# Hybrid decoder step on one core: the down projection of 15 pairs of ff tiles as seven products, with weights combined on the chip

## The reference, cut to what matters

```python
D_MODEL = 1024
SEQ = 2048
D_FF = ((8 * D_MODEL + 3 * 256 - 1) // (3 * 256)) * 256      # 2816 = 22 tiles of 128
...
    h = _rmsnorm(x, g_pre_ffn) * (1.0 + sc_f) + sh_f
    gate, up = jnp.split(jnp.einsum('btd,df->btf', h, w_ffn_in), 2, axis=-1)
    f = jnp.einsum('btf,fd->btd', jax.nn.silu(gate) * up, w_ffn_out)
    x = x + gt_f * _rmsnorm(f, g_post_ffn)
```

## Time and profile before

| | before |
|---|---|
| median of three runs | 2795.2 us |
| the profiled execution, its own time | 2790.03 us |
| its span, first to last instruction | 2788.1 us |
| outside the span | 1.9 us |
| TensorE busy, instructions | 2552.7 us (92%), 15508 matmuls |
| VectorE / ScalarE / GpSimd busy | 1742.2 (62%) / 1095.0 (39%) / 896.4 us (32%) |
| feed-forward part | about 1318 to 2781 us of the span |
| group 1's first product ends, group 2's | 1795.5 us, 2277.9 us |
| mean granted TensorE clock | 0.966 of full |

### The profile page before, as it was taken

One profiled execution on the slowest core, in us unless ns is written; L12 is line 12 of the kernel. 1 busy time (PEld: TensorE's weight loads), 2 busy tenths in 40 slices (PEclk: granted clock), 3 DMA queues, 4 the chain that ended last, 5 costly groups with the idle time before them and its releaser, 6 DMA issues.

```text
span 2788.1 us, 42200 instructions
## 1 busy us (share of the span) xinstructions
PE 2552.7 (92%) x15508; PEld 2388.6 (86%) x15508; DVE 1742.2 (62%) x2474; ACT 1095.0 (39%) x1921; POOL 896.4 (32%) x740
## 2 busy tenths in 40 slices
PE   5999999868888969997899999899999999999995
PEld 4999999747777757775899999899999999999995
DVE  3798779566776746745577777754444465444446
ACT  3545545357767764554433333340101124011012
POOL 2566567322323211001565565311212212122121
PEclk8999999979999989998999999999999999999998
DMA  7345345253333326965798787687657659576574
GB/s 259 113 159 188 121 157 182 74 124 86 93 94 97 99 70 195 276 202 147 282 345 309 290 323 288 234 269 261 236 195 249 241 175 300 200 253 236 195 249 134
DMA packets 262598, 557.60 MB, mean 200 GB/s; under 512 B 25266, under 2 KB 163506, under 8 KB 250626
## 3 DMA queue, kind: packets, MB, share of 16 engines
q1 hardware_dynamic: 189906, 331.19, 36.1%
q0 software_dynamic: 50688, 207.64, 21.6%
q10 hardware_dynamic: 21808, 16.09, 2.1%
HBM read 404.70 MB, written 150.18 MB: 199 GB/s over the span
## 4 chain that ended last, share of the span: by engine, by line
PE 40%; issue 4%; DVE 3%; DMA 3%; POOL 1%; ACT 1%; SPq 0%; DVEq 0%; ACTq 0%; POOLq 0%
PE p_z L2353 24%; PE p_y L2375 16%; DMA w_parts<-p_c 1%; DMA p_c<-w_parts 1%; DMA o_parts<-p_o 1%; POOL p_o L2298 1%; POOL p_c L2147 0%; DVE p_T_lo L2226 0%; DVE p_tt L2548 0%; DVE p_y L2597 0%; DVE ffn_wraw L2196 0%; DVE p_rstd L2590 0%; ACT p_o L2400 0%; DVE p_E L2219 0%; DVE p_E L2579 0%
## 5 line engine op out<-in xcount | busy, mean ns | idle before, releaser
L2353 PE MATMUL p_z<-p_T_hi,p_c 128*128 128x342 f32 (+1 forms) x3696 | 915.1, 323 | 20.3 <-PEq L1317 8.2
L2353 PEld LDWEIGHTS p_z<-p_T_hi,p_c 128*128 128x128 f32 x3696 | 655.6, 191 | 25.2 <-issue 15.6
L2353 PE MATMUL p_z<-p_T_lo,p_c 128*128 128x342 f32 (+1 forms) x1848 | 596.4, 323 | 0.0
L2375 PE MATMUL p_y<-p_f_hi,p_o 128*128 128x342 f32 (+1 forms) x2112 | 534.3, 323 | 20.6 <-POOL p_o L2298 7.4
L2375 PEld LDWEIGHTS p_y<-p_f_hi,p_o 128*128 128x128 f32 x2112 | 375.8, 191 | 25.3 <-issue 10.6
L2574 DVE TENSOR_TENSOR p_y<-p_y 128x342 f32<-128x342 f32 (+1 forms) x480 | 239.1, 509 | 198.7 <-PE p_y L2375 198.6
L359 POOL TENSOR_TENSOR p_w_lo<-p_wraw,p_w_hi 128x1024 fp32r<-128x1024 f32 x100 | 294.0, 2949 | 205.2 <-ACT p_w_hi L434 204.9
L2147 POOL DMA_DIRECT2D p_c<-w_parts x308 | 163.0, 530 | 607.2 <-PE p_z L2353 604.7
L2353 PEld LDWEIGHTS p_z<-p_T_lo,p_c 128*128 128x128 f32 x1848 | 352.2, 191 | 0.5 <-issue 0.2
L2375 PE MATMUL p_y<-p_f_lo,p_o 128*128 128x342 f32 (+1 forms) x1056 | 341.0, 323 | 0.0
L394 PE MATMUL p_proj<-p_h_hi,p_w_hi 128*128 128x412 f32 (+1 forms) x800 | 285.5, 357 | 8.8 <-DVE p_h_lo L612 8.7
(11 more groups left out here) (302 smaller groups left out, 4214.1 us busy)
## 6 DMA issues: line engine op xcount, KB each, us to landing
p_c<-w_parts POOLq DMA_DIRECT2D x308, 512.0 KB, 5.7
w_parts<-p_c SPq DMA_DIRECT2D x154, 512.0 KB, 4.3
p_wraw<-w_in SPq DMA_DIRECT2D x100, 512.0 KB, 4.8
p_o<-o_parts POOLq DMA_DIRECT2D x44, 1024.0 KB, 6.8
o_parts<-p_o SPq DMA_DIRECT2D x22, 1024.0 KB, 4.9
p_ada<-w_ada SPq DMA_DIRECT2D x32, 512.0 KB, 4.4
sq_group<-z SPq DMA_DIRECT2D x110, 128.0 KB, 3.2
p_graw<-w_ffn SPq DMA_DIRECT2D x11, 1024.0 KB, 7.0
```

Source lines behind the costliest of these rows:

```text
L2353: mm = pe.matmul(out[:, 0:W], c[r][:, a, k, :], b[j][:, k, 0:W], start=i == 0, stop=i == 11)
L2375: mm = pe.matmul(Y[q % YB][:, 0:W], o[s][:, a, m, :], b[s][:, n, 0:W], start=s == 0 and i == 0, stop=s == 1 and i == 2)
```

## The change

In group 1 the pairs 1 to 7 and in group 2 the pairs 1 to 8 (d = 24 to 36 and 46 to 60) are computed as seven products of 4 tiles with 3 matmuls each, 84 matmuls in place of 96. What goes into the products is made on the chip: on the side of f, VectorE makes four differences (`sum_f`: t1 to t4) and three more lo parts (`low_x`), and ScalarE three more hi parts; on the side of the weights, VectorE makes four sums of 128x512 (`sum_o`: s3, s1, s2, s4). The seven sums X are kept apart from y, three in y and four in E0 and E1, whose space h occupied; so h of the group after is loaded at t = 19 in place of 3 (group 0 still loads at 3). After the last such pair VectorE joins them by eight additions of 128x4x342 (`mix`). The tiles stand two behind each product of the units d+2 and d+3.

`o_parts` is gone. The down weights' hi and lo are no longer stored and loaded back: for all pairs of groups 1 and 2 the raw weights of a pair (1 MB) come into graw1 by SP's queue (`load_raw_o`), and ScalarE (L2513) and GpSimd (L2403) split them in parts of 128x512, seven for a pair of the new kind and four for the others. The others are 96 matmuls as before.

```diff
+SEVEN = {1: range(1, 8), 2: range(1, 9)}
...
-            pair = [("y", u - 2, n, m) for n in range(2) for m in range(KT)]
+            if seven(u - 2):
+                pair = [("p", u - 2, i, m) for i in range(NPR) for m in range(4)]
+            else:
+                pair = [("y", u - 2, n, m) for n in range(2) for m in range(KT)]
...
+    for d, Q in first_part.items():
+        e = NPR * (d + 2)
+        raw_at[d + 1] = d
+        for i, at in enumerate((-3, -1, 1, 2, 4, 6, 6) if seven(d) else (-4, -3, -2, 0)):
+            part_at.setdefault(divmod(e + at, NPR), []).append((d, i, Q + i))
+        for name, at in (("s3", -2), ("s1", -2), ("s2", -1), ("s4", 5)) if seven(d) else ():
+            sums_at.setdefault(divmod(e + at, NPR), []).append((d, name))
...
             for u in range(NU4):
                 G, t = group(u), u % FT
-                if 0 < u <= FT:
-                    store("o", u - 1)
-                    if u < FT:
-                        load_o(u)
+                if 0 < u < FT:
+                    load_o(u)
+                if u in raw_at:
+                    load_raw_o(raw_at[u])
...
-                if t == 3 and G + 1 < NGR:
+                if t == (19 if G else 3) and G + 1 < NGR:
...
             for u in range(NU4):
-                late = u > FT and u % FT == 3
-                if u and (u <= FT or u % 2) and not late:
+                if 0 < u <= FT:
                     low_o(u - 1)
...
+                for j in range(NPR):
+                    low_w(pool, NPR * u + 5 + j)
+                    low_parts(u, j)
...
+            def high_parts(u, j):
+                for d, i, Q in part_at.get((u, j), ()):
+                    wait_raw_o(act, d)
+                    if seven(d) and i in (1, 2, 3, 5):
+                        wait_o_sum(act, d, {1: "s1", 2: "s2", 3: "s3", 5: "s4"}[i])
+                    wait_tile(act, part_end[Q - 4] if Q >= 4 else done[FT - 2])
+                    act.activation(o_part(Q)[:, 0], part_of(d, i), ACT.Copy).then_inc(S["hi"], 1)
...
                 silu(u, 0)
+                high_parts(u, 3)
+                high_parts(u, 4)
                 if ends is not None:
                     root(ends, 0)
                     gate(ends, 1)
```

More of the change, by code:

```diff
@@ L1983, in ffn, with copied @@
         order.append(("sum", NGR - 1, n))
-    added = [sum(x[0] == "y" for x in order[:q + 1]) for q in range(len(order))]
-    done = {}
+    added = [sum(x[0] != "sum" for x in order[:q + 1]) for q in range(len(order))]
+    adds = [q for q, x in enumerate(order) if x[0] != "sum"]
+    def copied(q):
+        x = order[q]
+        return x[1] % FT == 0 or (x[0] == "p" and x[1] % FT == 2 and x[2] < 4)
+    turned = {q for p, q in zip(adds, adds[1:]) if copied(p) != copied(q)}
+    F_OF = [(0, 0), (0, 1), "t2", "t3", (1, 0), (1, 1), "t4"]
@@ new lines, in f_events @@
+    def f_events(u):
+        names = [("f", 0), ("lo", 0), ("f", 1)]
+        if not seven(u - u % 2):
+            return names + [("lo", 1)]
+        return names + (["t2", "t4", "t3", "lot2", "lot3", ("lo", 1), "lot4"] if u % 2 else ["t1", "lot1"])
+    f_at, count = {}, 0
+    for u in range(NU4):
+        for name in f_events(u):
+            count += 1
+            f_at[u, name] = count
+        f_at[u, "last"] = count
+    mix_at = {}
+    for G, r in SEVEN.items():
+        e = NPR * (FT * G + 2 * r[-1] + 2)
+        for i in range(8):
+            mix_at.setdefault(divmod(e + (8, 9, 11, 13, 14, 15, 16, 17)[i], NPR), []).append((G, i))
@@ L2465, in _ @@
                     high_o(u - 1)
+                high_parts(u, 0)
                 high_w(act, NPR * u + 5)
@@ L2473, in _ @@
                     root(late, 1)
+                if u % 2 == 0 and seven(u - 2):
+                    high_x(u - 2, "t2")
+                    high_x(u - 2, "t3")
                 for j in range(3):
@@ L2625, in _ @@
                     gated(u - 1, 1)
+                one = u - 1 if u % 2 and seven(u - 1) else None
+                two = u - 2 if u % 2 == 0 and seven(u - 2) else None
+                if one is not None:
+                    sum_f(one, "t1")
+                if two is not None:
+                    for name in ("t2", "t4", "t3"):
+                        sum_f(two, name)
                 collect(u, 0)
-                if u and not (G and t == 3):
+                if u and not (G and t == 3) and two is None:
                     low_f(u - 1, 1)
+                if two is not None:
+                    low_x(two, "t2")
                 if ends is not None:
@@ L2644, in _ @@
                 collect(u, 2)
+                if two is not None:
+                    low_x(two, "t3")
                 comb(u, "c11")
@@ L2647, in _ @@
                 comb(u, "u2")
-                if G and t == 3:
+                if (G and t == 3) or two is not None:
                     low_f(u - 1, 1)
@@ L2653, in _ @@
                 comb(u, "u4")
+                if two is not None:
+                    low_x(two, "t4")
                 if turn:
```

295 lines of the change are left out of this document (218 added, 77 removed).

## The result

The changed kernel took 2807.97 us (median of five runs, 2805.89 to 2815.91) against 2788.21 us (2784.74 to 2796.25) for the kernel before beside it: ratio 1.0071, 95% interval 1.0053 to 1.0088. It is slower by some 20 us. The profiled execution has a span of 2806.3 us, 18.2 more than before, at a mean granted clock of 0.959 (0.966 before).

The account below looks back on a forecast made before the run. TensorE's matmul chain was taken as the bound. Terms -28.4 - 6.0 - 1.0 + 6.0 + 0.7 + 35.8 = +7.1 us on the profiled 2790.0 gave 2797.1, as a median 2802 us (+0.25%), range 2786 to 2819.

Parts of the forecast that it names:

- Matmuls removed: Later groups: 15 pairs lose 12 matmuls each, 180 at 157.8 ns, -28.4 us if TensorE stays the bound.
- Stall at 1880: TensorE's stall at 1880 to 1900 us, 38 matmuls short, goes as h loads later: -6.0 us.
- The -1.0 in group 2: Same place in group 2 lacks 9 matmuls, 1.4 us; half the weight traffic remains, so -1.0 us was taken.
- Steady pairs: Seven-product pairs: a VectorE addition some 0.4 us late per pair, 15 times, +6.0 us; 0 if queue ops overlap.
- Joins: Eight VectorE joins per group over ten products, one late by 0.35 us: +0.7 us for two groups.
- Turns: Starts of groups 1 and 2: ScalarE and GpSimd wait for late raw weights, 17.9 us each, +35.8 us together.
- R: Time the raw down weights land at the turn into group 1, forecast 1851.0 us, 8.5 us after their load starts.
- "I add nothing" for the clock: Low granted clock after a TensorE stop: nothing added, since pauses stood there before.
- The first rival: Turns of the groups: delay under 10 us instead of 17.9 each, sum -8.7 us, kernel faster; chance 0.14.
- The turns don't cost: The first rival by its title: ScalarE's root and copies have slack at the turns, kernel faster; chance 0.14.
- VectorE becomes the bound: Rival, steady pairs: GpSimd lengthens VectorE's work to 40.2 us against 39.8, +12 us, 2814; chance 0.25.
- The raw weights land late: Rival, turns: raw weights take 15.8 us to land, turns cost 14.6 us more, 2817; chance 0.15.

Follow-up runs that it names:

- e2: Changed kernel, raw load still late, with GpSimd's four subtractions of d = 22 and 44 moved behind unit 24's (46's) second weight load: 2812.94 us, ratio 1.0077.
- e3: Changed kernel, raw load still late, with ScalarE's four copies of d = 22 and 44 moved to the start of unit 24 (46): 2794.17 us, ratio 0.9998.
- e1_raw_first: Changed kernel with the raw load of d = 22 and 44 queued one unit earlier, ahead of both loads of x: 2767.61 us, ratio 0.9907.
- e9: e1_raw_first plus one unused VectorE subtraction per seven-product pair, only ahead of the lo part of f at the predicted tightest place: 2783.94 us, ratio 0.9963.
- e5: e1_raw_first plus d = 42's parts later, raw load of d = 24 and 46 ahead of y's stores, four group 2 joins later: 2763.52 us, ratio 0.9892.
- e8: e5 with the parts of d = 42 back at their old places: 2770.01 us, ratio 0.9915.

## Why the prediction came out as it did

The direction and the cause were right: the time is in the range, above the predicted 2802, and slower by more than 0.3%, to which I had given 0.44. The size was not: +0.25% was forecast and +0.71% measured, and 2807.97 lies near 2802 only because the kernel before had a median 7 us lower beside it than the one I had added to. That the range was met is in part luck: terms too small or missing are some 18 us, and the 6.0 us that the steady pairs didn't cost took back a third of them. By the steps of the sum, in the profiled execution (18.2 us more in place of my 7.1):

- **Matmuls removed**, -28.4: a pair is 1.94 us shorter, 15 times, -29.1. Right.
- **Stall at 1880**, -6.0: unit 26 to 27 gains 5.6 beyond a pair's own step. Right. The -1.0 in group 2 became +1.2, as in e2 and e3, which have the late load too; in e1_raw_first it is -0.3. So most of that hangs on the late load, and how stays open.
- **Steady pairs**, +6.0: 0.0. The place was right and the size was off by 0.4 us a pair, since I priced each instruction at its length, 510 ns, while VectorE starts the next one 0.42 us later. I had named this as the lower bound. What was counted as 0.4 late is just in time; e9 shows that nothing is left there. GpSimd's subtraction does fall on this place, but it lengthens the sum of weights by 0.7 us, not the lo of f as I had counted.
- **Joins**, +0.7: 2.9, of which 2.2 in group 2 (below).
- **Turns**, +35.8: 41.2 (19.1 from unit 22 to 26, 22.1 from 45 to 48). The chain held row by row: R was 1853.20, u4 of unit 24 ended at R + 24.6 (I said R + 24), and VectorE's first addition moved by 20.4, which is 17.7 without the offset of 2.7, against my 17.9. The weights took 10.5 and 9.7 us to land, not 8.5. Mis-sized was what comes behind: "I add nothing" for the clock, whose mean was 0.69 and 0.76 in the windows of the turn (0.93 and 0.98 before), as units 25 and 26 lost 1.4 us more; and in group 2 the load of d = 46, behind both stores of y. e1_raw_first, which has no late load, still loses 2.7 us from unit 45 to 48; e5 and e8, which load d = 46 ahead of the stores, lose 1.9.
- **Not in the sum**: 3.8 us in units 43 to 45. There the four parts of d = 42 run beside the T splits, and two of VectorE's sums of T took 2.67 and 2.65 us (1.57 before). That this is the cause isn't shown: e5 moves these parts away and loses 1.6 us there, e8 leaves them and loses 1.1. And 2.7 us of offset, the spread between executions.

These are -29.1 - 5.6 + 1.2 + 0.0 + 2.9 + 41.2 + 3.8 + 2.7 = 17.1, and 1.1 behind the last unit.

Rivals. The first rival's "from about 9.5 us per turn downwards" doesn't fit its own sum, which passes the 8.4 us of a clear gain at 10.2 us per turn and zero at 14.4; nothing hangs on it here. *The turns don't cost*: false, and e1_raw_first shows that they would not have, had the load stood one unit earlier. *VectorE becomes the bound*: not in this kernel; in the steady pairs of group 1 TensorE waits for it once, 0.4 us, at their start; but e9 shows that one more instruction in the tightest excerpt makes it so. VectorE and GpSimd did lengthen each other as I feared, only more rarely. Here are two groups of VectorE by form, 1950 to 2109 us of the changed kernel, four pairs (busy us, mean ns, idle before):

```profile
L2705 DVE TENSOR_TENSOR p_cg<-p_cg,p_up 128x342 f32<-128x342 f32 x4 | 6.3, 1576 | 0.0
L2744 DVE TENSOR_TENSOR p_graw<-p_graw 128x512 f32<-128x512 f32 x4 | 5.5, 1365 | 0.0
```

Each is longer than alone (about 520 and 678) by 1.06 and 0.69 us, with a lo part of x (681 ns against 514, twice a pair) some 2.1 us a pair. The Trainium skill (SBUF — State Buffer, Who interferes with whom) has such instructions exclude each other, and each meeting in the trace agrees; read as every subtraction stopping VectorE for its whole length, it gave 9.3 us a pair, over four times what the trace has. *The raw weights land late*: 10.5 us, nearer to 8.5 than to 15.8.

The 2.2 us at the joins of group 2 are a meeting as well. VectorE's join and GpSimd's subtraction, in the changed kernel and below it in e9 (start us, us):

```profile
2708.96 1.28 POOL L2403 TENSOR_TENSOR p_o<-p_graw,p_o 128x512 fp32r<-128x512 f32 x1 [0.73 <-ACT p_o L2513]
2709.05 2.64 DVE L2763 TENSOR_TENSOR p_E<-p_E 128x1368 f32<-128x1368 f32 x1
```

```profile
2686.44 1.58 DVE L2774 TENSOR_TENSOR p_E<-p_E 128x1368 f32<-128x1368 f32 x1
2686.70 2.46 POOL L2403 TENSOR_TENSOR p_o<-p_graw,p_o 128x512 fp32r<-128x512 f32 x1 [0.72 <-ACT p_o L2513]
```

In the changed kernel GpSimd starts 0.09 us earlier and the join takes 2.64 us in place of 1.58; TensorE then waits 1.9 us for the addition behind it. In e9, with the same joins, VectorE starts first, GpSimd's subtraction is the longer one, TensorE waits 0.4 us and the stretch costs 0.7.

## What to carry to other kernels

When a load is added to an in-order queue, look at what stands ahead of it there and what that waits for, then at what stands behind its first reader on each engine; here one position was worth 40 us, more than all the matmuls removed. The longest wait that the profile names need not set the time: opening it alone (e2) gained nothing, because a second chain from the same late load was longer (e3). A dose of one small instruction at the place that the count calls tightest, and the same everywhere else, tells whether an engine's sum or its order is near the bound.

## What the runs showed of the hardware

- VectorE can begin the next instruction 0.42 us after one whose own row says 0.51 (the lo part at 2008.83, the addition at 2009.26 and the sum at 2009.68 above). Where the next one waits for the one before, it is 0.60: the additions of unit 24 in the kernel before start at 1854.62, 1855.22 and 1855.83. A count of in-order work goes by the distance between starts, not by the length of rows. The busy time of a window, 30.6 us in 40 in e1_raw_first from 1940 on, counts such an overlap once.
- Where VectorE and GpSimd meet in SBUF, the one that starts later is lengthened: the join by 1.06 us behind GpSimd's start, GpSimd's subtraction by 1.2 behind VectorE's, in the rows above. In unit 43 GpSimd's subtraction (2267.65) took 2.20 us in place of 1.31 behind a lo part of VectorE (2267.13), and VectorE's next sum (2268.62) 2.67 in place of 1.57 behind that subtraction.
- A short wait can cost more than itself, and does not always. In e1_raw_first the addition behind the join holds TensorE 1.86 us at 2671, and this window has 45 matmuls where its neighbour has 65:

```profile
2670.00:2680.00 10.00, 8.63 (x45) 8.63 (x46) 8.55 (x14) 2.56 (x5) 2.39 (x3) 0.83 0.43 116
2680.00:2690.00 10.00, 10.00 (x65) 10.00 (x64) 8.72 (x13) 0.49 (x1) 1.58 (x3) 1.00 0.87 303
```

  The same wait in the changed kernel (2710 to 2720 us) leaves 52 matmuls at a clock of 1.00. The stretch costs 3.7 us in e1, e2 and e3, 2.1 to 2.2 in the changed kernel, e5 and e8: the 1.5 us between them are the clock's. What decides between the two is open.
- The load of raw down weights, 6.9 us to landing in the median of e1_raw_first, took 10.2 us (1873.26 to 1883.48) and 15.5 us (2336.78 to 2352.24) where it was issued right behind the two stores of y, and 10.5 and 9.7 us behind the two loads of x in the changed kernel. In e1_raw_first loads of c were under way as well, so what each did to it isn't separated.
